# Lower halves of the weights on another engine, and the MLP's squares formed in PSUM

## The reference, cut to what matters

```
hn = rms(h, g_mlp_pre[i])
y = jnp.square(jax.nn.relu(hn @ w_mlp_in[i])) @ w_mlp_out[i]
h = h + rms(y, g_mlp_post[i])
```

## Time and profile before

| | us |
|---|---|
| runs (3) | 2676.33, 2682.53, 2687.46 |
| median | 2682.53 |
| span of the profiled execution | 2678.6 |

### The profile page before, as it was taken

How to read it: one execution, slowest core, us unless ns; L and a number is a source line. 1 busy time by engine, 2 the same in 40 slices (tenths; PEclk the granted TensorE clock), 3 DMA queues, 4 the chain that set the end, 5 groups by cost and what they waited for, 6 DMA issues and landing times.

```text
span 2678.6 us, 27715 instructions
## 1 busy us (share of the span) xinstructions
PE 2057.1 (77%) x11128; PEld 1282.3 (48%) x11128; DVE 957.7 (36%) x1639; ACT 675.0 (25%) x1110; POOL 729.6 (27%) x309
## 2 busy tenths in 40 slices
PE   5999978789976665665556656657779898998898
PEld 3766866667963111111111111117649784657874
DVE  3364577785463000000000000006647612456712
ACT  3243234444431000000000000013334421353431
POOL 2432256555742000000000000005216650114670
PEclk7999889999986788778887787778889998998999
DMA  7634134444545999999999999993315454314452
GB/s 265 226 103 139 42 89 92 95 109 113 179 148 208 416 417 418 418 418 418 418 418 417 417 417 418 418 379 109 120 32 162 151 172 160 126 32 134 157 173 98
DMA packets 221794, 619.00 MB, mean 231 GB/s; under 512 B 9008, under 2 KB 104624, under 8 KB 188928
## 3 DMA queue, kind: packets, MB, share of 16 engines
q1 hardware_dynamic: 216048, 598.32, 58.6%
q0 software_dynamic: 4832, 16.19, 3.5%
q10 hardware_dynamic: 816, 3.15, 0.3%
HBM read 616.52 MB, written 1.11 MB: 231 GB/s over the span
## 4 chain that ended last, share of the span: by engine, by line
PE 44%; DMA 31%; DVE 16%; issue 5%; ACT 3%; POOL 1%; SPq 0%; POOLq 0%; DVEq 0%; ACTq 0%
DMA ring<-in_w_edown 10%; DMA ring<-in_w_eup 10%; DMA ring<-in_w_egate 9%; PE bank L471 8%; PE bank L472 7%; PE bank L473 7%; DVE work L2090 4%; PE bank L1942 4%; PE bank L2128 2%; PE bank L1959 2%; PE bank L560 2%; DVE work L1574 1%; PE bank L531 1%; PE bank L1046 1%; PE bank L1375 1%
## 5 line engine op out<-in xcount | busy, mean ns | idle before, releaser
L454 POOL TENSOR_TENSOR ring_parts<-ring,ring_parts 128x2048 fp32r<-128x2048 f32 (+2 forms) x129 | 577.5, 4484 | 1425.8 <-ACT ring_parts L448 1402.5
L1942 PE MATMUL bank<-ring,work 128*32 128x512 f32 x2048 | 327.0, 771 | 225.5 <-DMA ring<-in_w_eup 140.3
L2002 DVE TENSOR_TENSOR work<-bank,work 128x512 f32<-128x512 f32 x16 | 11.1, 692 | 915.0 <-PE bank L1942 915.0
L448 ACT CAST ring_parts<-ring 128x2048 fp32r<-128x2048 f32 (+2 forms) x137 | 251.5, 1845 | 176.6 <-DMA ring<-in_w_mlp_out 78.1
L1942 PEld LDWEIGHTS bank<-ring,work 128*32 128x32 f32 x2048 | 64.1, 126 | 478.8 <-issue 179.0
L1959 PE MATMUL bank<-ring,work 128*32 128x512 f32 x1024 | 177.6, 828 | 124.3 <-DMA ring<-in_w_edown 118.2
L471 PE MATMUL bank<-hn_hi,ring_parts 128*128 128x256 f32 x640 | 188.6, 295 | 34.6 <-ACT work L2074 23.1
L471 PE MATMUL bank<-hT_hi,ring_parts 128*128 128x256 f32 (+1 forms) x576 | 199.9, 347 | 7.8 <-POOLq L295 4.0
L472 PE MATMUL bank<-hT_lo,ring_parts 128*128 128x256 f32 (+1 forms) x576 | 189.9, 330 | 0.0
L473 PE MATMUL bank<-hT_hi,ring_parts 128*128 128x256 f32 (+1 forms) x576 | 189.7, 329 | 0.0
L472 PE MATMUL bank<-hn_lo,ring_parts 128*128 128x256 f32 x640 | 184.4, 288 | 0.0
(11 more groups left out here) (356 smaller groups left out, 3350.6 us busy)
## 6 DMA issues: line engine op xcount, KB each, us to landing
ring<-in_w_egate SPq DMA_DIRECT2D x64, 2048.0 KB, 16.7
ring<-in_w_eup SPq DMA_DIRECT2D x64, 2048.0 KB, 16.5
ring<-in_w_edown SPq DMA_DIRECT2D x64, 2048.0 KB, 17.1
ring<-in_w_in SPq DMA_DIRECT2D x36, 1024.0 KB, 7.2
ring<-in_w_mlp_in SPq DMA_DIRECT2D x32, 1024.0 KB, 5.3
ring<-in_w_mlp_out SPq DMA_DIRECT2D x32, 1024.0 KB, 5.0
ring<-in_w_ada SPq DMA_DIRECT2D x12, 2048.0 KB, 12.2
ring<-in_w_ab SPq DMA_DIRECT2D x12, 1024.0 KB, 5.1
```

The source lines that it names most:

```text
L448: act.copy(halves_of(name, ring_parts)[1], halves_of(name, ring)[0]).then_inc(hi_made, 1)
L454: pool.tensor_tensor(lo, halves_of(name, ring)[0], hi, ALU.subtract).then_inc(lo_made, 1)
L1942: last = pe.matmul(bank[which][32 * n:32 * n + 32, :], xg[:, e2, 2 * c + k2, :], w[:, k2, 512 * n:512 * n + 512], start=c == 0 and k2 == 0 ...
```

## The change

1. Lower halves go from POOL to DVE in the projections of both attentions (`na_proj_dve`: after every second rope; `ab_proj_dve`: likewise, and four for v), in the merge (`merge_dve`: three early ones, then one after every second `na` block and two after every second `ssd` block, the rest at the end) and in both MLPs (all of them, one per pair of blocks). `na_proj_pool`, `merge_pool` and `mlp_pool` go.
2. Where POOL keeps them (modulation, during the neighbourhood attention, SSD, the two units ahead of each MLP, `aq_0`, `aq_1`), it works in pieces of 512 columns: four instructions for a unit of 2048 columns, with one semaphore at the last.
3. MLP: ACT's `Relu` no longer frees the bank. DVE multiplies bank and `hid_r` into the same bank, ACT rounds from the bank, DVE subtracts from the bank and frees it. `hid_sq` goes. ACT's `split_upper` comes behind the pair's blocks, DVE's `split_lower` behind them too.
4. The two memsets of `qz_ab` go from DVE to POOL, behind `aq_1` and the load of `grow`.

```diff
-        def split_lower(pool, name):
+        def split_lower(dve, name):
             lo, hi = halves_of(name, ring_parts)
+            dve.wait_ge(hi_made, SPLIT.index(name) + 1)
+            dve.tensor_tensor(lo, halves_of(name, ring)[0], hi, ALU.subtract).then_inc(lo_made, 1)
+
+        PIECE = 512
+
+        def split_lower_pool(pool, name):
+            lo, hi = halves_of(name, ring_parts)
+            whole = halves_of(name, ring)[0]
+            _, kt, n, _ = chunks[CHUNK[name]]
             pool.wait_ge(hi_made, SPLIT.index(name) + 1)
-            pool.tensor_tensor(lo, halves_of(name, ring)[0], hi, ALU.subtract).then_inc(lo_made, 1)
+            for c in range(0, kt * n, PIECE):
+                ins = pool.tensor_tensor(lo[:, c:c + PIECE], whole[:, c:c + PIECE], hi[:, c:c + PIECE], ALU.subtract)
+            ins.then_inc(lo_made, 1)
...
         def na_proj_dve(dve, hf):
                 rope_dve(dve, tb("na_qc"), tb("na_qs"), [(qz[0:64, b, 0, :], 0, 64), (qz[64:128, b, 1, :], 64, 128)])
+                if b % 2:
+                    split_after(split_lower, dve, f"q{hf}_{b // 2}")
...
         def merge_dve(dve):
+            merge_splits = iter(MERGE_UNITS)
             grow_dve_in(dve, 0, gdiag4)
+            split_after(split_lower, dve, f"gates_{EARLY_GATES // 2 - 1}")
             dve.wait_ge(o_rounded, 1)
             dve.tensor_tensor(oT_lo[:, :, :], oT, oT_hi[:, :, :], ALU.subtract).then_inc(o_made, 1)
+            split_after(split_lower, dve, "gates_6")
...
             grow_out(dve.tensor_copy, dve, 0)
+            split_after(split_lower, dve, "gates_7")
             for i in range(8):
...
                 dve.tensor_tensor(uT[:, i, :], bank[n % 4][:, 0:L], gT[:, i, :], ALU.mult).then_inc(gemm_freed, 1)
+                if i % 2:
+                    split_next()
             for i in range(8):
...
                 dve.tensor_tensor(uT_lo[:, i, :], uT[:, i, :], uT_hi[:, i, :], ALU.subtract).then_inc(merged, 1)
+                if i % 2:
+                    split_next()
+                    split_next()
+            for name in merge_splits:
+                split_lower(dve, name)
...
         def mlp_act(act, l):
             split_upper(act, units[SPLIT_EARLY])
+            def round_hid(m):
+                n = GROUP[f"up{l}"] + m
+                act.wait_ge(hid_squared, 32 * l + m + 1)
+                act.copy(hid_hi[:, m, :], bank[n % 4][:, 0:L]).then_inc(hid_rounded, 1)
             for i in range(UPS):
-                split_upper(act, units[i + SPLIT_EARLY + 1])
...
-                    act.activation(hid_r[:, m % 2, :], bank[n % 4][:, 0:L], ACT.Relu).then_inc(gemm_freed, 1)
+                    act.activation(hid_r[:, m % 2, :], bank[n % 4][:, 0:L], ACT.Relu).then_inc(hid_relu, 1)
                     if m >= 1:
-                        act.wait_ge(hid_squared, 32 * l + m)
-                        act.copy(hid_hi[:, m - 1, :], hid_sq[:, (m - 1) % 2, :]).then_inc(hid_rounded, 1)
+                        round_hid(m - 1)
+                split_upper(act, units[i + SPLIT_EARLY + 1])
...
         def mlp_dve(dve, l):
-            for m in range(33):
-                if m < 32:
-                    dve.wait_ge(gemm_freed, GROUP[f"up{l}"] + m + 1)
-                    if m >= 2:
-                        dve.wait_ge(hid_made, 32 * l + m - 1)
-                    dve.tensor_tensor(hid_sq[:, m % 2, :], hid_r[:, m % 2, :], hid_r[:, m % 2, :], ALU.mult).then_inc(hid_squared, 1)
-                if m >= 1:
-                    dve.wait_ge(hid_rounded, 32 * l + m)
-                    dve.wait_ge(hid_squared, 32 * l + m)
-                    dve.tensor_tensor(hid_lo[:, m - 1, :], hid_sq[:, (m - 1) % 2, :], hid_hi[:, m - 1, :], ALU.subtract).then_inc(hid_made, 1)
...
+            def lower_hid(m):
+                n = GROUP[f"up{l}"] + m
+                dve.wait_ge(hid_rounded, 32 * l + m + 1)
+                dve.tensor_tensor(hid_lo[:, m, :], bank[n % 4][:, 0:L], hid_hi[:, m, :], ALU.subtract).then_inc(gemm_freed, 1)
+            for i in range(UPS):
+                for m in (2 * i, 2 * i + 1):
+                    b = bank[(GROUP[f"up{l}"] + m) % 4][:, 0:L]
+                    dve.wait_ge(hid_relu, 32 * l + m + 1)
+                    dve.tensor_tensor(b, b, hid_r[:, m % 2, :], ALU.mult).then_inc(hid_squared, 1)
+                    if m >= 1:
+                        lower_hid(m - 1)
+                split_lower(dve, units[i + SPLIT_EARLY + 1])
+            lower_hid(2 * UPS - 1)
+            for u in units[UPS + SPLIT_EARLY + 1:]:
                 split_lower(dve, u)
...
         def ab_proj_pool(pool):
-            split_lower(pool, "ak_0")
             for t in "ab":
-                for m in "qkv":
-                    for u in range(2):
-                        ab_split(split_lower, pool, f"{t}{m}_{u}")
+                pool.memset(qz_ab[t], 0.0).then_inc(qz_zero, 1)
...
                     rope_dve(dve, tb("ab_qc"), tb("ab_qs"), [(q[0:64, b, 0, :], 0, 64), (q[64:128, b, 1, :], 64, 128)])
+                    if b % 2:
+                        ab_split(split_lower, dve, f"{t}q_{b // 2}")
```

More of the change, by code:

```diff
@@ L762, in ada_pool @@
         def ada_pool(pool):
-            split_after(split_lower, pool, "ada1")
+            split_after(split_lower_pool, pool, "ada1")
             for k in range(0, KT, 2):
@@ L1327, in ssd_pool @@
         def ssd_pool(pool):
-            split_after(split_lower, pool, "dt")
-            split_after(split_lower, pool, "xs0_0")
+            split_after(split_lower_pool, pool, "dt")
+            split_after(split_lower_pool, pool, "xs0_0")
             pool.wait_ge(at_done, 1)
@@ L1336, in ssd_pool @@
                     for name in ("xs0_1", "b0", "c0"):
-                        split_after(split_lower, pool, name)
+                        split_after(split_lower_pool, pool, name)
                 if n >= 2:
@@ L1355, in ssd_pool @@
             for u in range(2, EARLY_GATES // 2 - 1):
-                split_after(split_lower, pool, f"gates_{u}")
+                split_after(split_lower_pool, pool, f"gates_{u}")
         def product(pe, g, r):
@@ L1762, in merge_dve, with split_next @@
             link = stepper(dve, dve_step)
+            merge_splits = iter(MERGE_UNITS)
+            def split_next():
+                split_lower(dve, next(merge_splits))
             grow_dve_in(dve, 0, gdiag4)
+            split_after(split_lower, dve, f"gates_{EARLY_GATES // 2 - 1}")
             dve.wait_ge(o_rounded, 1)
             dve.tensor_tensor(oT_lo[:, :, :], oT, oT_hi[:, :, :], ALU.subtract).then_inc(o_made, 1)
+            split_after(split_lower, dve, "gates_6")
             for i in range(2):
@@ L2013, in build @@
         rm = Region(HID + 2 * DFF // P * L)
-        hid_r, hid_sq = rm.take(2, L), rm.take(2, L)
+        hid_r = rm.take(2, L)
         tmpm = xnm.rearrange("p t (h n) -> p (t h) n", h=2)
@@ L2084, in mlp_dve @@
         def mlp_dve(dve, l):
[L2085 to L2098 removed]
+            units = units_of(l)
+            dve.wait_ge(lo_made, SPLIT.index(units[SPLIT_EARLY]))
+            split_lower(dve, units[SPLIT_EARLY])
+            def lower_hid(m):
[3 more added lines that the diff above has]
+            for i in range(UPS):
+                for m in (2 * i, 2 * i + 1):
+                    b = bank[(GROUP[f"up{l}"] + m) % 4][:, 0:L]
[6 more added lines that the diff above has]
+            for u in units[UPS + SPLIT_EARLY + 1:]:
                 split_lower(dve, u)
@@ L2101, in mlp_dve @@
             close_dve(dve, MLP + 3 * l, tmpm)
-        def mlp_pool(pool, l):
-            for u in units_of(l)[SPLIT_EARLY:-2]:
-                split_lower(pool, u)
         def split_early_act(act, l):
@@ L2112, in split_early_pool @@
             for u in units_of(l)[:SPLIT_EARLY]:
-                split_lower(pool, u)
+                split_lower_pool(pool, u)
         def load_grow(pool, i):
@@ L2210, in ab_split @@
                 split_after(split, eng, name)
+        qz_zero = sem("qz_zero")
         def ab_proj_pool(pool):
[L2213 removed]
             for t in "ab":
[L2215 to L2217 removed]
+                pool.memset(qz_ab[t], 0.0).then_inc(qz_zero, 1)
         def ab_proj_act(act):
@@ L2237, in ab_proj_dve @@
             link = stepper(dve, dve_step)
-            link(dve.memset(qz_ab["a"], 0.0))
-            link(dve.memset(qz_ab["b"], 0.0))
+            dve.wait_ge(lo_made, SPLIT.index("ak_0"))
+            split_lower(dve, "ak_0")
             dve.wait_ge(tab_in, 16)
-            for t in "ab":
+            for i, t in enumerate("ab"):
+                dve.wait_ge(qz_zero, i + 1)
                 for b in range(4):
@@ L2244, in ab_proj_dve @@
                     rope_dve(dve, tb("ab_qc"), tb("ab_qs"), [(q[0:64, b, 0, :], 0, 64), (q[64:128, b, 1, :], 64, 128)])
+                    if b % 2:
+                        ab_split(split_lower, dve, f"{t}q_{b // 2}")
                 for b in range(4):
```

(13 more changed lines are left out.)

34 lines of the change are left out of this document (9 added, 25 removed).

## The result

The changed kernel takes 2601.68 us (median of 4 runs, 2599.13 to 2609.41) against 2682.27 (4 runs, 2676.33 to 2687.46): a ratio of 0.971, 95% interval 0.9688 to 0.9731. The forecast was 2618 with 2600 to 2650. The gain is 80.6 us instead of 64.6; on the profiled executions it is 2678.6 - 2600.5 = 78.1.

A forecast was written before the change was run, and what follows sets the result against it. It took POOL's splits, holding DVE while PE waits, as the bound where PE idles. Terms 28 + 7.6 + 12 + 10 + 2.5 + 5 - 0.5 = 64.6 took the span from 2678.6 to 2614.0; plus 3.9, 2618 us (2600 to 2650).

The forecast's parts named there:

- POOL's splits hold DVE, and one instruction gets through between two of POOL's: Everywhere: DVE instructions with two SBUF inputs wait up to 4.6 us per POOL split, one passing between POOL instructions.
- MLP up, 28: MLPs' up part: PE sets the pace, a pair taking 5.76 us instead of 7.21; 14 us won per MLP.
- The bank's way (2.5 us to spare): MLPs' up part: DVE frees the odd bank at T + 6.1 us, PE wants it at T + 8.64.
- the ring rival: MLPs' up part: ACT and DVE's ring binds, a pair takes 6.5 us, 7 won per MLP; 2632 us, chance 0.13.
- MLP down, 7.6: MLPs' down part: PE's two waits for POOL's splits, 3.8 us together per MLP, vanish; 7.6 us for two MLPs.
- Merge, 12: Merge's end: 10.3 us from PE's shorter wait after the last `ssd` block and 1.8 from the clock, together 12.
- Projections of block two, 10: Block two's projections: PE's waits of 10.4 us for `raw` and 1.0 for a split; 10 won, 12 with the clock.
- Attention, 2.5: Both attentions: steps have one held DVE instruction, which waits 1.3 us instead of 4.6 with pieces; 2.5 us won.
- SSD, 5: SSD stage: shorter holds by POOL's pieces, on a mask's wait and elsewhere, win 5 us (bounds -12 and +10).
- POOL's end, +0.5: End of the SSD stage: POOL's last split takes 0.5 us longer, a loss.
- SSD didn't get worse with pieces: Rival for SSD: pieces let DVE delay POOL's decays, 22 us lost where 5 were won; 2645 us, chance 0.09.
- the waits pass to DVE's queue: Rival for merge and block two: ropes and evictions queue behind DVE's splits, their gains lost; 2640 us, chance 0.09.

The follow-up runs named there:

- mlp_psum: The changed kernel, but POOL forms the MLPs' lower halves in whole units as before, squares still formed in PSUM: 2600.57 us, ratio 0.9688.
- pieces_only: The kernel before, changed only so that POOL forms each lower half in pieces of 512 columns: 2617.52 us, ratio 0.9748.
- after_whole: The changed kernel, but POOL forms each lower half it still has in one instruction: 2621.15 us, ratio 0.9768.

## Why the prediction was right, and where its sizes were off

- *POOL's splits hold DVE, and one instruction gets through between two of POOL's*: right, shown by mlp_psum and by the turns in pieces_only.
- *MLP up, 28*: 27.0. PE sets the pace. The bank's way (2.5 us to spare) held, but the 1.8 us of idle DVE that I set against the ring rival was the wrong measure: the loop of ACT and DVE has 0.9. And each of three edits without the other two (the move, PSUM, the pieces) gives the whole 27: I had put it down to an idle POOL. The move and PSUM were run with ACT's new order, which by itself gives nothing; in the old order they weren't run.
- *MLP down, 7.6*: 11.1. All of it lies in the first 120 matmuls, which took 33.6 and 32.0 us in the two MLPs and now take 27.3. The two late units are gone, as foreseen, but the term was taken from PE's idle time alone. From start to start of the matmuls around them they cost some 4.7 per MLP, not 3.8, and the first MLP also ran part of this stretch (2130 to 2149) at a clock of 0.91.
- *Merge, 12*: 12.6. The wait is 10.5 shorter, as worked out. `out` and the router take 2.7 less, 1.8 of it in the first 52 matmuls, at 1.00. This clock term came in this execution, but after_whole and two others wait as short and start at the lower clock: that part was luck as much as forecast.
- *Projections of block two, 10*: 15.4. The term was too small. PE idles 11.3 us less, which is the two waits that the forecast named, 10.4 and 1.0, and took 10 of. PE's own work takes 4.1 less, at a clock of 0.98 instead of 0.93, and for this the forecast put nothing; its "12 with the clock" was too little. DVE's queue did not bite.
- *Attention, 2.5, SSD, 5, POOL's end, +0.5*: 3.5 and 3.4 in this pair of executions. But after_whole loses 19, of which 16 are left without `out`, the router and the experts, where these terms say 7: this term was mis-sized. Nine executions with pieces of 512 on POOL in SSD lie between 382.6 and 391.8 (mean 387.3), two with whole units at 393.4 and 397.4: 8 us in the mean, and 3.4 is one draw of it.
- *Modulation*, no term at all, though it has the same hold: 4.3. PE waited there too, 4.2 us, behind a DVE instruction held by POOL's split. Ten executions with pieces of 512 lie from 53.6 to 57.1 (mean 55.5), three with longer ones at 57.8 or 57.9, so some 2.4 are the pieces' in the mean. The three at 53.6 and 53.7, the changed kernel among them, are those in which DVE's two small instructions began before POOL's first piece; in the other seven one of them takes 1.2 us.
- The rivals: the ring didn't bind, SSD didn't get worse with pieces (and much better with shorter ones), nor did the waits pass to DVE's queue.

So the time fell 16 below the forecast. 13.5 of it are in the profiled spans: 5.4 of block two, 4.3 of modulation, 3.5 of the MLPs' down part and small ones of either sign. The other 2.7 are the step from span to median, which was 1.2 instead of 3.9. The mechanism was right and several sizes were too small on the same side. 2601.68 is near the range's low end, and that end is not well founded: SSD at 10 instead of 5, projections 2 and MLPs 4 more make 11 us, which gives 2607 and not 2600. By its own terms the measured time would lie outside, so that it lies inside is partly luck.

Open: why SSD takes one of two levels in the same code (382.6 to 383.1 in three executions, 387.8 to 391.8 in six). PE's own work is part of it, 343.0 to 344.0 us in the three and 346.7 to 349.3 in the six. Open as well: why the clock behind the merge's short wait is sometimes the lower one.

## What to carry to other kernels

Where a DVE instruction is many times its usual length and ends with one of POOL, there are three cures, and any of them may be enough: move POOL's work to DVE, bring one operand of DVE's from PSUM, or cut POOL's instruction so that DVE gets as many turns as it needs, but no finer than POOL's own time allows. Moving it is worth trying even where DVE looks dense, since part of its busy time is waiting. The room for more work is what the longest loop through the engines leaves, not an engine's idle time.

## What the runs showed of the hardware

- In pieces_only POOL and DVE took strict turns when both had conflicting instructions ready: 1.44 us per piece of 512 columns with one DVE instruction of 256 columns each, against 4.62 for the whole 2048 at once.
- A subtraction of 2048 columns takes POOL 4.6 us whole; in four pieces of 512 with DVE out of the way 5.0 (1.25 each); in pieces of 256 with DVE's turns 6.2.
- DVE writes a product into the very bank that it reads in 0.429 us for 256 columns, against 0.422 from SBUF to SBUF.
